# Two transformer blocks on one core: the passes of the high halves first behind each turn, merged rows turned inside a block's last quarter, the second expert's first split moved

## The chip, the core and the metric

The kernel runs on one core of a Trainium2 chip. TensorE (PE) multiplies, VectorE (DVE), ScalarE (ACT) and GpSimd (POOL) do the rest, SyncE (SP) issues nearly all loads. The metric is the device time of one execution in microseconds.

## The reference

Two blocks are computed on 256 tokens of width 1024, everything in float32. The outline of `reference()`:

```
first_block:  h = rms_norm(x); z = h @ w_in                      # 5.9k columns
              differential attention (8 heads) -> @ w_proj_a     # "pa"
              latent attention (8 heads)       -> @ w_proj_b     # "pb"
              merged = sigmoid(g_a)*y_a + sigmoid(g_b)*y_b
              x += rms_norm(merged @ w_o)                        # "wo"
              x += rms_norm((silu(h @ gate) * (h @ up)) @ down)  # FFN, 2816 wide
second_block: u = modulate(rmsnorm(h), shift, scale); z = u @ w_in_2        # "jn"
              retention -> @ w_ret_out ("ro"), sparse attention -> @ w_dsa_out ("do")
              h += g1 * ((ga*y_ret + gb*y_dsa) @ w_o)                        # "xo"
              t = modulate(rmsnorm(h)); router picks 2 of 16 experts a token
              h += g2 * sum_e gate_e * ((silu(t @ w1_e) * (t @ w3_e)) @ w2_e)
              return rmsnorm(h, norm_final_g)
```

## The kernel before, in words

**Three passes for one product.** A float32 product is made of three matmuls on rounded operands: high half of the rows by high half of the weights, high by low, low by high. `three` (L2387, L2388, L2389) issues these three side by side for each 128-row K tile. The high half of a weight unit (128 x 1024, two K tiles of 512 columns) is a copy on ACT (L986, L980), the low half a subtraction on DVE (L1522, L1517) that follows it. A unit passes through a ring of four slots; `used` counts units that PE is done with.

**A turn.** Before rows can be multiplied they are transposed: PE turns a token tile of 128 rows in two groups of four 128 x 128 transposes (L2496), ACT takes the high half out of PSUM (`rows_hi`, L1079), DVE the low half (`rows_lo`, L1657, L1659). `pairs_freed` makes PE wait until the low half is there, and `lo_ready` until the low half of the unit is. So the first product behind a turn waits for PE, ACT and DVE in a row.

**Blocks by rows.** Six places have a turn behind work that ends late. There PE takes token tile 0 through all four units first, turns the rows of tile 1 in between, and then takes tile 1 (`block_by_rows`, and `first_gate_up` for the FFN and for the first expert). The places are `x1` (start), `mg` (merged rows, block wo0), `x2` (FFN), `u` (block jn0), `mh` (merged rows, block xo0) and `v` (expert 0). The merged rows of token tile 0 are ready in the middle of block pb1 (do1), but PE turns them when this block is over.

**The order on ACT and DVE** is written by hand: each engine's program calls `split_to(n)` to say how many units are split before the next other step. It is not planned by costs, and the queues run strictly in that order. ACT before wo0 splits three units ahead and then takes the turned rows.

**The experts.** Expert 0's load is fixed; those from the second on are placed by the router's answer (`bases`), so SP issues them only when this is known. Beside expert 1's first products PE gathers the tokens of the small groups in eight steps (L2963, L2964), each into one PSUM bank: step n+1 waits until ACT has copied (L1434) and DVE has subtracted (L2296) step n. ACT and DVE work on the router (L1460 to L1463, L2245 to L2265) between the splits of the second expert's units; `L1463` is a dummy that loads the Silu table again behind the two Exp.

## Time and profile before

| | us |
|---|---|
| median of 3 runs (1011.11 to 1012.3) | 1011.11 |
| the profiled execution: its own time | 1013.72 |
| its span in the profile | 1012.1 |
| PE busy in it (92%) | 934.3 |
| DVE busy / ACT busy / POOL busy | 691.0 / 523.4 / 247.0 |

Start times in rows count from the start of the span; around the span lie 1.62 us. The two remaining views that matter are the timeline, in which a bracket behind an instruction tells how long its engine sat idle before it and what ended that, and the granted clock by stretch (1.00 is 2.4 GHz, 0.50 is 1.2 GHz).

### The profile page before, as it was taken

What the parts mean: (1) busy time and instruction counts of PE and PEld (TensorE: products, weight loads), DVE (VectorE), ACT (ScalarE), POOL (GpSimd) and SP (SyncE); (2) the same over time, 40 slices, a digit from 0 to 9 for tenths busy, and PEclk for the clock granted to TensorE, in tenths of its full rate; (3) what the DMA queues carried; (4) which work ended last, traced back from release to release, by engine and by line L of the source; (5) the groups of instructions that cost most, each with busy time, mean ns of one, the idle gap of its engine ahead of it and who ended that gap; (6) DMA issues with size and microseconds to landing.
All of it is one profiled execution on the core that took longest, in us unless ns stands there. A gap on an engine that the chain in (4) does not pass through costs nothing. (4 is left out here: it accounts for less than half of the span.)

```text
span 1012.1 us, 12623 instructions
## 1 busy us (share of the span) xinstructions
PE 934.3 (92%) x4334; PEld 748.1 (74%) x4334; DVE 691.0 (68%) x933; ACT 523.4 (52%) x814; POOL 247.0 (24%) x228
## 2 busy tenths in 40 slices
PE   4998999889998999999989998998989989999995
PEld 3886776678775888888678885686767768777774
DVE  4868467857756687878665443896667875785973
ACT  4655566665346353434444555544434464674661
POOL 3686036599522011110127000023100100000001
PEclk9999999999999999999989999898999999999998
DMA  8646846546555799997547655243235184996951
GB/s 274 202 138 187 274 119 201 166 140 214 192 167 197 254 299 325 299 325 252 165 124 201 195 168 168 91 146 105 84 110 187 56 278 143 320 317 231 325 203 41
DMA packets 116148, 199.45 MB, mean 197 GB/s; under 512 B 6361, under 2 KB 63761, under 8 KB 115841
## 3 DMA queue, kind: packets, MB, share of 16 engines
q1 hardware_dynamic: 110192, 177.00, 53.9%
q0 software_dynamic: 5904, 21.78, 6.5%
q8 instruction: 29, 0.48, 0.2%
q14 instruction: 23, 0.19, 0.1%
HBM read 197.70 MB, written 2.62 MB: 198 GB/s over the span
## 5 line engine op out<-in xcount | busy, mean ns | idle before, releaser
L1522 DVE TENSOR_TENSOR w_lo<-raw,w_hi 128x1024 fp32r<-128x1024 f32 x220 | 288.8, 1325 | 137.0 <-ACT w_hi L986 134.4
L2387 PE MATMUL lin<-w_hi,a_hi 128*128 128x512 f32 (+2 forms) x728 | 293.4, 403 | 18.3 <-DVE w_lo L1522 6.6
L986 ACT ACTIVATE w_hi<-raw 128x1024 fp32r<-128x1024 f32 x220 | 229.3, 1058 | 123.6 <-PE lin L2389 116.8
L2389 PE MATMUL lin<-w_hi,a_lo 128*128 128x512 f32 (+2 forms) x728 | 284.7, 391 | 0.0
L2388 PE MATMUL lin<-w_lo,a_hi 128*128 128x512 f32 (+2 forms) x704 | 274.7, 390 | 0.0
L2387 PEld LDWEIGHTS lin<-w_hi,a_hi 128*128 128x128 f32 x728 | 139.9, 192 | 53.1 <-issue 14.9
L2389 PEld LDWEIGHTS lin<-w_hi,a_lo 128*128 128x128 f32 x728 | 139.8, 192 | 29.4
L2388 PEld LDWEIGHTS lin<-w_lo,a_hi 128*128 128x128 f32 x704 | 135.2, 192 | 25.0
L858 POOL TENSOR_SCALAR stat<-stat 128x2 f32<-128x2 f32 (+1 forms) x31 | 11.4, 368 | 511.6 <-ACT idk_t L1099 451.9
L2496 PE MATMUL turn<-cst,arena 128*128 128x128 f32 x230 | 35.0, 290 | 22.0 <-DVE arena L1711 10.0
L2387 PE MATMUL lin<-w_hi,b_hi 128*128 128x512 f32 x114 | 46.3, 407 | 4.8 <-DVE arena L1559 2.0
L2496 PEld LDWEIGHTS turn<-cst,arena 128*128 128x128 f32 x230 | 26.8, 147 | 32.3 <-DMA cst<-in_constants_dram 7.9
L906 POOL TENSOR_SCALAR rows<-rows,c_col 128x1024 f32<-128x1024 f32 x16 | 48.8, 3049 | 2.2 <-POOL mod L907 1.5
L925 POOL DMA_DIRECT2D arena<-in_w_ada_dram x32 | 16.9, 529 | 125.1 <-DVE mod L1616 124.6
L2389 PE MATMUL lin<-w_hi,b_lo 128*128 128x512 f32 x114 | 45.2, 397 | 0.0
L907 POOL TENSOR_TENSOR mod<-mod,rows 128x1024 f32<-128x1024 f32 x16 | 41.9, 2620 | 1.3
L1616 DVE SCALAR_TENSOR_TENSOR mod<-arena,c_col,mod 128x1024 f32 x32 | 40.9, 1278 | 0.0
L1117 ACT ACTIVATE probs<-sco,stat 128x128 f32<-128x128 f32 (+1 forms) x48 | 19.6, 419 | 36.3 <-DVE stat L1681 36.3
L2388 PE MATMUL lin<-w_lo,b_hi 128*128 128x512 f32 x94 | 37.4, 398 | 0.0
L1079 ACT ACTIVATE a_hi<-turn 128x512 fp32r<-128x512 f32 x24 | 13.2, 595 | 40.8 <-PE turn L2496 40.8
L2387 PE MATMUL lin<-w_hi,arena_r 128*128 128x512 f32 x80 | 32.6, 407 | 0.0
L2389 PE MATMUL lin<-w_hi,arena_r 128*128 128x512 f32 x80 | 31.5, 394 | 0.0
(434 smaller groups left out, 1601.7 us busy)
## 6 DMA issues: line engine op xcount, KB each, us to landing
raw<-in_w_in_dram SPq DMA_DIRECT2D x76, 512.0 KB, 4.4
arena<-in_w_ada_dram POOLq DMA_DIRECT2D x32, 512.0 KB, 5.9
raw<-in_w_ffn_gate_dram SPq DMA_DIRECT2D x22, 512.0 KB, 5.0
raw<-in_w_ffn_up_dram SPq DMA_DIRECT2D x22, 512.0 KB, 6.1
raw<-in_w_ffn_down_dram SPq DMA_DIRECT2D x22, 512.0 KB, 4.0
rows<-in_w_ada_dram SPq DMA_DIRECT2D x16, 512.0 KB, 4.0
raw<-in_w_o_dram SPq DMA_DIRECT2D x16, 512.0 KB, 4.1
raw<-in_w_gate_dram SPq DMA_DIRECT2D x16, 512.0 KB, 4.0
```

The lines of the kernel that those rows point to most:

```text
L906: step(pool.tensor_scalar(early_slots[n % 3], early_slots[n % 3], c_col[:, k:k + 1], None, ALU.mult))
L907: pool.tensor_tensor(acc, acc, early_slots[n % 3], ALU.add).then_inc(ada_done, 1)
L925: pool.dma_start(ada_slots[k % 4], ada_source(k, bass.ds(i * D + 2 * D, D)))\
L986: act.activation(w_hi[:, s, :], raw[:, s, :], ACT.Copy).then_inc(hi_ready, 1)
L1079: act.activation(a_hi[:, 4 * (g % 2):4 * (g % 2) + 4, t * P:(t + 1) * P], bank_of(f"{label}.{g}").rearrange("p (k n) -> p k n", k=4), ACT. ...
L1117: i = act.activation(dst, src, ACT.Exp, bias=st("nmax", k, 1), accum_out=st("rsum", k, 1))
L1522: dve.tensor_tensor(w_lo[:, s, :], raw[:, s, :], w_hi[:, s, :].bitcast(F32), ALU.subtract)\
L1616: dve.scalar_tensor_tensor(out=acc, in0=ada_slots[k % n_s], scalar=c_col[:, k:k + 1], in1=acc, op0=ALU.mult, op1=ALU.add).then_inc(ada_don ...
L2387: pe.matmul(dst, l_hi, r_hi, start=start, stop=False)
L2388: pe.matmul(dst, l_hi, r_lo, start=False, stop=False)
L2389: return pe.matmul(dst, l_lo, r_hi, start=False, stop=stop)
L2496: i = pe.transpose(b[0:n, at:at + m], src, ident[0:m, 0:m])
```

## The change

At the places above PE issues the high-by-high passes by themselves (`unit_high`, waiting only for the high halves) and the other two passes later (`unit_rest`). `turned_block` writes this order out for the blocks behind a turn; the first block of the FFN, expert 0 (token tile 0), the product do0, expert 1 and the two last down products get the same split. The merged rows of tile 0 are turned before the last unit of pb1 (do1). Two of the four sums of shift rows move ahead of the turn of tile 1 in the FFN. On ACT and DVE `split_to` calls and the steps around them move accordingly. In expert 1 the high half of its first unit is made between the two Exp, its low half before the end of the router's arithmetic, and the table load comes after the splits of the first gate and up units.

```diff
+HI_NAMES = [n for n in TURN_NAMES if TURNS[n][1] == "dve" and n[:3] not in ("dao", "dso")]
+HI_MADE = {name: count + 1 for count, name in enumerate(HI_NAMES)}
...
             u_next = BLOCKS["wo0"][1]
-            split_to(u_next + LEAD)
+            split_to(u_next + 2)
             rows_hi("mg", 0, 0.5)
...
             rows_hi("x2", 0)
+            squares("wo.1", [lin[:, b + 1, :] for b in banks])
             split_to(u_next + 4)
-            squares("wo.1", [lin[:, b + 1, :] for b in banks])
             rows_hi("x2", 1)
+            shift_copied(0, 2)
...
             act.activation(route_x, route_x, ACT.Exp).then_inc(route_e, 1)
+            split_to(u + 1)
             act.wait_ge(route_in, 2)
             act.activation(route_y, route_y, ACT.Exp).then_inc(route_e, 1)
-            act.activation(st("route", 30, 1), st("neg_half", 0, 1), ACT.Silu)
             split_to(u + 2)
             side(0, "down")
             split_to(u + 4)
+            act.activation(st("route", 30, 1), st("neg_half", 0, 1), ACT.Silu)
...
-                split_to(u_next + 1)
+                split_to(u_next + 2)
+                rows_lo(label, 0, 0.5)
                 dve.wait_ge(used, u_next)
                 merge_rows(name, gate, 1)
-                rows_lo(label, 0, 0.5)
...
             dve.wait_ge(first_rows, 2)
+            wo_weighted(0)
             wo_rows(0)
-            split_to(u_next + LEAD - 1)
+            split_to(u_next + 2)
             rows_lo("x2", 0)
+            dve.wait_ge(used, u_next)
+            wo_weighted(1)
+            split_to(u_next + 3)
+            wo_rows(1)
             split_to(u_next + 4)
-            dve.wait_ge(used, u_next)
-            wo_rows(1)
             rows_lo("x2", 1)
...
             add_normed("ffn", 1)
+            rows_lo("u", 0)
             dve.wait_ge(x_ready, 2 * NT)
             step(gained(1, mod[:, D:2 * D]))
-            rows_lo("u", 0)
...
             first_of(per(r_em, 16), cst[:, C_W16:C_W16 + 16], 16, m)
+            split_to(gate_up_unit(1) + 1)
             dve.wait_ge(route_e, 2)
...
+                if name == "do0":
+                    if part == 0:
+                        for p in range(2):
+                            pe.wait_ge(turn_hi, HI_MADE[f"de.{p}"])
+                            for t in range(NT):
+                                unit_high(name, p, t)
+                    pairs_freed(f"de.{part}")
+                    for t in range(NT):
+                        unit_rest(name, part, t)
+                    return
...
+            def turned_block(name, label, *rows_from):
...
+                    for part in range(3):
+                        high(part, 0)
+                    rest(0, 0)
+                    rest(1, 0)
+                    high(3, 0)
+                    rest(2, 0)
+                    turn_second(label, *rows_from)
+                rest(3, 0)
+                high(0, 1)
+                high(1, 1)
+                for part in range(4):
+                    rest(part, 1)
+                    if part < 2:
+                        high(part + 2, 1)
...
-            block_by_rows("pb1")
-            turn_first("mg", NT + 1, gate1, merged)
-            block_by_rows("wo0", "mg", NT + 1, gate1, merged)
+            block_by_rows("pb1", lambda: turn_first("mg", NT + 1, gate1, merged))
+            turned_block("wo0", "mg", NT + 1, gate1, merged)
...
+                            if (t, half) == (0, 1):
+                                shift_sums(0, 2)
+                                turn_second(rows_label, count)
                             pairs_freed(f"{rows_label}.{2 * t + half}")
...
+                    if p == 1:
+                        for t in range(NT):
+                            gate_up_high(t, u, half)
                     pe.wait_ge(lo_ready, u + 2 * half + 2)
```

What this does on PE between block pb1 and block wo0 (`turn` is the turned merged rows, `mod` their source, `arena_r` the left operand of pb1, `a_hi` and `a_lo` that of wo0). Before, from the end of pb1:

```order
L2387 MATMUL lin<-w_hi,arena_r 128x512
L2388 MATMUL lin<-w_lo,arena_r 128x512
L2389 MATMUL lin<-w_hi,arena_r 128x512
L2496 MATMUL turn<-cst,mod 128x128 x8
L2387 MATMUL lin<-w_hi,a_hi 128x512
L2388 MATMUL lin<-w_lo,a_hi 128x512
L2389 MATMUL lin<-w_hi,a_lo 128x512
```

Now, from the same turn:

```order
L2578 MATMUL turn<-cst,mod 128x128 x8
L2399 MATMUL lin<-w_hi,arena_r 128x512
L2400 MATMUL lin<-w_lo,arena_r 128x512
L2401 MATMUL lin<-w_hi,arena_r 128x512
L2399 MATMUL lin<-w_hi,arena_r 128x512
L2400 MATMUL lin<-w_lo,arena_r 128x512
L2401 MATMUL lin<-w_hi,arena_r 128x512
L2470 MATMUL lin<-w_hi,a_hi 128x512 x6
L2479 MATMUL lin<-w_lo,a_hi 128x512
L2480 MATMUL lin<-w_hi,a_lo 128x512
```

Six matmuls of pb1 stand behind the turn now, and six passes that need only high halves come before the first low one.

On ACT beside the router: `stat` is the router's row, `w_hi<-mod` are the high halves of expert 1's first four units, `arena_r<-turn` is the copy of the first gathered step, `mod<-lin` the scaled result of expert 0. Before:

```order
L1460 ACT_TABLE_LOAD
L1460 ACTIVATE stat<-stat 128x8
L1462 ACTIVATE stat<-stat 128x2
L1463 ACT_TABLE_LOAD
L1463 ACTIVATE stat<-stat 128x1
L980 ACTIVATE w_hi<-mod 128x1024 x2
L1434 ACTIVATE arena_r<-turn 128x384
L980 ACTIVATE w_hi<-mod 128x1024 x2
L1474 ACTIVATE mod<-lin,stat 128x512 x2
```

Now:

```order
L1465 ACT_TABLE_LOAD
L1465 ACTIVATE stat<-stat 128x8
L984 ACTIVATE w_hi<-mod 128x1024
L1468 ACTIVATE stat<-stat 128x2
L984 ACTIVATE w_hi<-mod 128x1024
L1439 ACTIVATE arena_r<-turn 128x384
L984 ACTIVATE w_hi<-mod 128x1024 x2
L1472 ACT_TABLE_LOAD
L1472 ACTIVATE stat<-stat 128x1
L1480 ACTIVATE mod<-lin,stat 128x512 x2
```

One split has moved ahead of the second Exp, and the table load from before four splits to behind them.

## Rows read from the trace of the kernel before

**Rows 1.** The page, busy time of the engines: us, share, instructions.

```profile
PE 934.3 (92%) x4334; PEld 748.1 (74%) x4334; DVE 691.0 (68%) x933; ACT 523.4 (52%) x814; POOL 247.0 (24%) x228
```

**Rows 2.** The waits, PE: in total, times, longest (us).

```profile
PE lin L2387 <- DVE a_lo L1657: 6.3, 3, 2.2
```

**Rows 3.** The timeline of PE, wo0, wo1: start, length, instruction, [idle before].

```profile
281.34 0.47 PE L2387 MATMUL lin<-w_hi,a_hi 128*128 128x512 f32 x1 [1.28 <-issue]
...
286.69 0.48 PE L2387 MATMUL lin<-w_hi,a_hi 128*128 128x512 f32 x1
...
304.56 1.09 PE L2496 MATMUL turn<-cst,arena 128*128 128x128 f32 x8
```

**Rows 4.** The timeline of PE and DVE, from the FFN to block jn0.

```profile
507.10 1.24 PE L2496 MATMUL turn<-cst,arena 128*128 128x128 f32 x8 [2.01 <-DVE arena L1716]
...
510.49 0.77 PE L2387 MATMUL lin<-w_hi,a_hi 128*128 128x512 f32 x1 [2.14 <-DVE a_lo L1657]
...
512.68 1.28 DVE L1716 SCALAR_TENSOR_TENSOR arena<-arena,stat,mod 128x1024 f32<-128x1024 f32 x1 [0.72 <-POOL stat L859]
...
516.66 1.03 PE L2496 MATMUL turn<-cst,arena 128*128 128x128 f32 x8
```

**Rows 5.** By stretch: busy PE, PEld, DVE, ACT, POOL; granted clock; DMA.

```profile
743.50:746.80 3.30, 3.30 (x9) 2.65 (x8) 1.29 (x2) 0.00 (x0) 0.00 (x0) 0.50 0.39 134
815.20:818.50 3.30, 3.30 (x9) 2.52 (x9) 3.19 (x7) 3.30 (x6) 0.00 (x0) 0.50 1.11 365
```

**Rows 6.** The timeline of DVE, block in0.

```profile
27.51 2.40 DVE L1522 TENSOR_TENSOR w_lo<-raw,w_hi 128x1024 fp32r<-128x1024 f32 x2
```

**Rows 7.** The timeline of PE and ACT, the FFN's first products.

```profile
307.63 0.47 PE L2387 MATMUL lin<-w_hi,a_hi 128*128 128x512 f32 x1 [1.97 <-DVE a_lo L1657]
...
314.15 1.10 PE L2496 MATMUL turn<-cst,arena 128*128 128x128 f32 x8 [2.12 <-DVE arena L1711]
...
321.50 1.28 ACT L1246 ACT_TABLE_LOAD   x1
...
321.92 1.88 PE L2555 MATMUL sco<-mod,ones 128*128 128x512 f32 x4
...
326.00 0.60 PE L2724 MATMUL turn<-cst,arena 128*128 128x128 f32 x4
```

**Rows 8.** The timeline of PE, the FFN's last down product.

```profile
495.92 0.50 PE L2387 MATMUL lin<-w_hi,b_hi 128*128 128x512 f32 x1 [1.41 <-DVE b_lo L1931]
```

**Rows 9.** The timeline of PE at block do0.

```profile
743.17 0.53 PE L2387 MATMUL lin<-w_hi,b_hi 128*128 128x512 f32 x1 [2.01 <-DVE arena L1559]
```

**Rows 10.** The timeline of PE, expert 0.

```profile
786.35 0.47 PE L2387 MATMUL lin<-arena_r,a_hi 128*128 128x512 f32 x1 [2.20 <-DVE a_lo L1657]
...
790.84 1.25 PE L2496 MATMUL turn<-cst,arena 128*128 128x128 f32 x8 [0.28 <-DVE arena L1716]
```

**Rows 11.** The timeline of SP, ACT, PE and DVE, expert 1's first half.

```profile
803.92 0.39 SPq L709 DMA_DIRECT2D mod<-in_w_exp_gate_dram  x1
...
810.10 1.28 ACT L1463 ACT_TABLE_LOAD   x1
...
811.50 1.99 ACT L980 ACTIVATE w_hi<-mod 128x1024 fp32r<-128x1024 f32 x2
...
814.99 0.70 PE L2387 MATMUL lin<-w_hi,a_hi 128*128 128x512 f32 x1 [3.22 <-DVE mod_r L1517]
...
817.94 1.93 ACT L980 ACTIVATE w_lo<-arena 128x2048 fp32r<-128x2048 f32 x1
...
822.63 0.55 DVE L2296 TENSOR_TENSOR arena_r<-turn,arena_r 128x384 fp32r<-128x384 f32 x1
...
823.23 0.45 PE L2963 MATMUL turn<-arena_r 128*128 128x384 f32 x1 [0.16 <-DVE arena_r L2296]
```

**Rows 12.** DMA issues from 800 to 816 us: median us from issue to landing.

```profile
mod<-in_w_exp_gate_dram SPq DMA_DIRECT2D x2, 512.0 KB, 5.2
...
rows<-in_w_exp_up_dram SPq DMA_DIRECT2D x1, 512.0 KB, 9.9
```

156 lines of the change are left out of this document (118 added, 38 removed).

## The prediction, written before the changed kernel ran

> **What bounds the kernel now.** I read the page first: PE is busy for 934.3 of 1012.1 us [rows 1], so PE bounds the kernel, and an edit can only win what PE does not do in the other 78 us, or what it does at half clock. Then the waits of PE: the longest lines are not loads but single steps of the chain turn, high half, low half, as the wait for `a_lo` with 3 cases and 6.3 us [rows 2]. Then the timeline at each turn, for what stands before and behind the wait, and last the granted clock around it. One matmul of 512 columns costs 0.229 us in a stream: 78 of them lie between 286.69 and 304.56 [rows 3]. At half clock it is 0.43 us: 18 between 510.49 and 516.66 took 6.17 us in place of 4.12, because most of them ran at the lower level [rows 4], and a busy stretch of 3.3 us at 0.50 did 9 [rows 5].
>
> The number of matmuls does not change; each edit is priced by how much earlier PE passes the place. Where PE streams before and after a place, loads and splits follow PE's `used` count and DVE's splits, so they shift with it, and a gain is kept.
>
> **Part by part.**
>
> Start (x1). PE's order gains some tenths, but the next block needs the low half of its first unit, and DVE makes that at 27.51 [rows 6] behind small work for tables that hangs on squares and loads, not on PE. I take 0; bounds 0 and 0.5 (two passes at 0.229 moved past the turn).
>
> Merged rows (mg, wo0). Before, PE sat 1.28 us at 281.34, and from there to 286.69 it did 18 matmuls (4.12) and one turn (0.8 without its tail; the row at 304.56 gives 1.09 with it) in 5.35, so another 0.4 was waiting [rows 3]. Now six matmuls, 1.4 us, lie behind the turn, and six high passes, 1.4 us, before the first low one. In these 2.8 us ACT makes two halves and DVE two differences of 0.6 each, which fit. The merge of tile 1 on DVE (2 x 0.7) comes behind them and is wanted only by the turn 20 passes later. So the whole 1.7 us goes. The lower bound is 1.0, if the third unit's split on ACT, now behind the turned rows, holds the sixth high pass. The same place in the second block (mh, xo0) has the same 1.28 us idle; merged(0) comes 0.3 us late for the earlier turn but the rest covers it: 1.6, at least 0.8.
>
> FFN's first products (x2). PE idles 1.97 us for the low half and 2.12 for the rows of tile 1 [rows 7]. The high passes fill the first, but the rows of tile 1 hang on squares, a POOL power and DVE, and I get their turn only 1.0 us earlier; the fourth unit's low half now comes behind them (0.4 of wait again). What counts is that two of the four sums, 1.88 us at 321.92 [rows 7], move into the wait at 314.15. Next in line is the table load at 321.50 that ends at 322.78, plus four instructions of 256 columns (0.4 each, estimated from 1.28 for 1024 columns [rows 4]), with the load 0.4 earlier than now: the turn of 326.00 can go at 324.3. I take 1.7; bounds 0.4 (only the load's shift) and 2.4.
>
> The last down products. Both wait 1.41 us for `b_lo` [rows 8] (two places, the second at 996.46). Four high passes (0.9) start when ACT's copy is there, one DVE difference (0.7) before the low half: 0.7 each; bounds 0.4 and 0.9.
>
> Rows u (jn0). PE waits 2.01 us for the modulated rows, which stays, then 2.14 us for `a_lo`, and runs the first part at half clock until 516.66 [rows 4]. With the highs at once PE starts 2.1 us earlier, at 508.4. The next bound is the modulated row of tile 1, 512.68 + 1.28 = 513.96. At full clock 20 passes end at 513.0 and the turn goes at 514.0, with 20 passes done where before 18 were done at 516.66: 2.66 + 0.46, less 0.35 for the fourth unit's low half, 2.75. With the clock falling exactly as before it is 1.1. The remaining idle is half as long, so a shorter low stretch is likely: I take 2.3.
>
> do0. PE idles 2.01 us because DVE evacuates block ro1 before `b_lo` [rows 9]; now eight high passes (1.8 us) need only ACT, which leaves 0.4 idle: 1.6. Behind the idle time PE was busy for a low stretch, 3.3 us at 0.50 [rows 5], which costs half of itself, 1.65. With 0.4 idle it should not come; I take 1.4 of it: 3.0; bounds 0.7 and 3.3.
>
> Expert 0 (v). The 2.20 us at 786.35 is filled in part, but the turn of tile 1 at 790.84 waits for DVE's rows [rows 10], so only the four extra high passes are won, 0.9. The router's arithmetic behind it is DVE's and not moved: I take 0.5; bounds 0 and 0.9.
>
> Expert 1. PE idles 3.22 us until 814.99 for `mod_r`, the low half whose high half ACT starts at 811.50 [rows 11]. Now the highs start at 811.3 and the lows at 813.8. But the eight gathers share one PSUM bank, and the third one waits for ACT and DVE. Their work is only re-ordered: of ACT's 1.28 us table load none goes away, it stands now before expert 0's result. I get ACT's pair of splits from 817.94 to 817.7, and then 1.93 for it, 2.4 for DVE's pair [rows 6] and 0.55 for the gather's difference (as at 822.63): the third gather at 822.6 in place of 823.23 [rows 11], 0.7 with the 0.5 of expert 0 in it. PE, being faster, arrives there at 818.2 and idles 4.3 us in one piece. Before, the 3.22 us were followed by a stretch at 0.50 from 815.2 to 818.5 [rows 5], and the wait at the third gather was still only 0.16 [rows 11]: that low stretch lay in DVE's shadow. The next one lies behind the third gather, where PE is what all wait for: half of 3.3, 1.65. Both experts together: 0.7 - 1.65 = -1.0; bounds -2.0 (a low stretch longer by one half) and +1.1.
>
> Here the split of three passes has a price that the trace must rule out. PEld counts 4334 loads for 4334 matmuls [rows 1]: each matmul has a load of its own already, so taking the two products of one left tile apart adds none. The Trainium skill (TensorE: Matmul & The Clock Gate, "What a matmul computes" and the step LDWEIGHTS) describes the load as its own instruction so that one load may serve many matmuls; by that rule some 120 left tiles would be loaded a second time. The trace disagrees for this kernel.
>
> The moved table load: the load at 810.10 takes 1.28 and ends at 811.38, the next activations come right behind, the split at 811.50 [rows 11]. No other cost shows. The Trainium skill (ScalarE: Activation LUTs, "What ACT_TABLE_LOAD costs") adds a drain of about 1380 ns to 1283 ns for a switch. By it the load in its new place would hold expert 0's result for longer; a mechanism of that kind is the fourth rival.
>
> **The sum.** 0 + 1.7 + 1.6 + 1.7 + 0.7 + 0.7 + 2.3 + 3.0 - 1.0 = 10.7 us off the profiled execution of 1013.72, which gives 1003.0. That execution stands 2.6 above the median of 1011.11, for which I have no cause in the program; the change of 10.7 is taken off the median: 1000.4.
>
> **The rivals.**
>
> 1. The clock spares expert 1 and block jn0: +1.65 and +0.45: 998.3. For it: after 1.97 and 2.12 us of idle time at 307.63 and 314.15 matmuls ran on at their usual step; against it: 3.22 us was followed by a low stretch.
> 2. The waits only move: DVE and ACT have their strict order, and behind the highs PE waits for the same low halves. Then the filled waits of x2 and u give nothing, since their ends hang on the rows of tile 1: without 1.7, 2.3 and half of do0's 3.0 the sum is 5.2: 1005.9. For it: five of the places end on DVE. Against it: the loss at half clock in [rows 4].
> 3. It does not do what it says: every high pass won is waited away before the low ones, since units' low halves come at DVE's rate, 2.4 us for two [rows 6], against 2.7 us that PE needs for one of twelve passes. PE is the slower, so I give little: 1010.5.
> 4. The table load costs as much again as its row shows, 1.28 us [rows 11], at a place where it stands between matmul results that ACT must fetch; the third gather comes that much later: 1001.7. Against it: at 810.10 nothing shows behind it.
> 5. Slower: expert 1's loads arrive late. SP issues them at 803.92, and the first split now stands before the second Exp in ACT's queue; behind it are queued the second Exp, on which the router's gates on DVE wait, the gather's copy and expert 0's result. The median landing of such a load is 5.2 us, 809.1, at most 0.4 late. But the slowest in the stretch took 9.9 [rows 12]: 813.8, 5.1 later than 808.7, when ACT would be free; this passes to the gathers, 4.4 after slack, with 2.5 of half clock. It decides from a landing later than 809.4 on. With the other terms at their lower ends (1.0 + 0.8 + 0.4 + 0.8 + 1.1 + 0.7 = 4.8) the kernel is 2.1 slower: 1013.2.
> 6. Slower by the weights: each of the 120 parted passes shows its load, 748.1 / 4334 = 0.17 us [rows 1], 20 in all: 1020.8. With loads hidden as now, nothing.
>
> **How the numbers follow.** Forecast 0.5 (1000.4, own range 998.9 to 1003), rival 1 0.15, rival 2 0.18, rival 3 0.04, rival 4 0.05, rival 5 0.05, rival 6 0.03. The range reaches from 997.5, below rival 1, to 1006, with rival 2 in it; outside are rivals 3, 5 and 6 and the tails, under 0.2. A measurement of this kernel can tell 0.2%, 2 us, from no change. Faster by more than 2 us are the forecast and rivals 1, 2 and 4: 0.88. Within it is rival 3 with half of rival 5: 0.06. Slower are the other half and rival 6: 0.06.
>
> **What would show it.** PE's idle time before the first product of wo0 and xo0 is gone (1.28 before). The turn of tile 1 in jn0 stands 2 to 3 us nearer to the turn of tile 0, and no low stretch follows do0. The hidden rows' first turn in the FFN comes right behind two sums, not four. Most telling is expert 1: a wait of about 4 us before the third gather, with a low stretch behind it, and a wait of 0.5 before the first low pass. Were there no wait, or an ACT queue that waits for a load before the second Exp, my order of events there would be wrong. If the total moves by less than 5 us although these waits are gone, the claim that a gain is kept through the streams is wrong.

## The result, and the profile after

The changed kernel took 1001.52 us (median of 4 runs, 1001.07 to 1003.31) against 1011.7 us for the kernel before on the same chip (4 runs, 1011.11 to 1013.55): ratio 0.9893, 95% interval 0.9879 to 0.9907. Forecast were 1000.4 us and a range from 997.5 to 1006.0. On a second chip it took 999.98 against 1013.81, ratio 0.9859 (0.9843 to 0.9875). The profiled execution took 1001.17 us with a span of 999.5, against 1013.72 and 1012.1 before. So the gain is 10.2 us by the medians of the first chip, 13.8 by those of the second, and 12.55 by the two profiles. Why these differ is a part of the finding.

From the page of the changed kernel, the busy time of the engines, which answers to [rows 1]:

```profile
PE 932.6 (93%) x4334; PEld 745.4 (75%) x4334; DVE 689.2 (69%) x933; ACT 523.1 (52%) x814; POOL 247.0 (25%) x228
```

There are as many matmuls and loads of left tiles as before, 4334 each, and both are busy for no longer. Taking the passes apart cost no load.

The timeline of PE after the change (start, length, instruction, [idle before, and what ended it]), from the merged rows to the FFN's hidden rows; it answers to [rows 3] and [rows 7]:

```profile
277.83 1.03 PE L2578 MATMUL turn<-cst,mod 128*128 128x128 f32 x8
...
280.10 1.53 PE L2470 MATMUL lin<-w_hi,a_hi 128*128 128x512 f32 x6
...
302.88 1.09 PE L2578 MATMUL turn<-cst,arena 128*128 128x128 f32 x8
304.48 1.17 PE L2776 MATMUL lin<-w_hi,a_hi 128*128 128x512 f32 x4 [0.51 <-ACT a_hi L1083]
...
308.60 1.88 PE L2637 MATMUL sco<-mod,ones 128*128 128x512 f32 x4
...
322.38 0.66 PE L2823 MATMUL turn<-cst,arena 128*128 128x128 f32 x4 [0.81 <-DVE arena L1921]
```

Six matmuls stand between the turn and the first high passes of wo0 (278.62 to 280.10), and none of the 1.28 us of idle time is left. The turn of the FFN's rows comes 1.68 us earlier than before, with 0.21 us lost ahead of the place: the step gave 1.89. Two of the four sums, 1.88 us, now stand at 308.60, where PE would wait for the rows of tile 1, and only two are left ahead of the hidden turn. PE's wait of 1.97 us before the first product of the FFN is one of 0.51 for the high half. The hidden turn comes 3.62 earlier, so the FFN's step gave 1.94.

The same view at u and jn0, which answers to [rows 4]:

```profile
502.79 1.09 PE L2578 MATMUL turn<-cst,arena 128*128 128x128 f32 x8 [2.00 <-DVE arena L1722]
504.33 1.62 PE L2470 MATMUL lin<-w_hi,a_hi 128*128 128x512 f32 x6 [0.45 <-ACT a_hi L1083]
...
509.85 1.09 PE L2578 MATMUL turn<-cst,arena 128*128 128x128 f32 x8 [0.62 <-DVE arena L1722]
```

The wait of 2.14 us for `a_lo` is now one of 0.45 for the high half, and the turn of tile 1 follows 7.06 us behind that of tile 0, where it was 9.56.

By stretch (length; busy PE, PEld, DVE, ACT, POOL; granted clock, DMA share, GB/s), in the kernel before behind the turn of u:

```profile
508.00:514.60 6.60, 4.46 (x12) 3.29 (x11) 5.81 (x7) 3.94 (x7) 1.41 (x2) 0.50 0.18 48
```

And in the changed kernel, behind the turn of u and behind that of de, where before had 0.50 in the first line of [rows 5]:

```profile
508.00:512.00 4.00, 3.34 (x18) 2.38 (x17) 3.25 (x4) 1.09 (x2) 0.47 (x1) 1.00 0.43 133
...
736.00:740.00 4.00, 4.00 (x20) 3.27 (x19) 2.42 (x4) 1.33 (x2) 0.00 (x0) 1.00 0.40 139
```

The timelines in expert 1 answer to [rows 11]. ACT:

```profile
803.38 1.28 ACT L1472 ACT_TABLE_LOAD   x1
804.67 0.20 ACT L1472 ACTIVATE stat<-stat 128x1 f32<-128x1 f32 x1
```

PE there:

```profile
803.54 0.50 PE L3007 MATMUL lin<-mod_r,a_hi 128*128 128x512 f32 x1 [0.79 <-DVE mod_r L1523]
...
811.91 0.44 PE L3086 MATMUL turn<-arena_r 128*128 128x384 f32 x1 [3.67 <-DVE arena_r L2308]
...
822.34 0.66 PE L3153 MATMUL turn<-cst,arena 128*128 128x128 f32 x4 [0.95 <-DVE arena L2290]
```

DVE, with the pair's split and behind it the difference that the third gather waits for:

```profile
809.10 2.29 DVE L1523 TENSOR_TENSOR arena_r<-arena,w_lo 128x2048 fp32r<-128x2048 f32 x1 [0.36 <-ACT w_lo L984]
811.31 0.55 DVE L2308 TENSOR_TENSOR arena_r<-turn,arena_r 128x384 fp32r<-128x384 f32 x1
```

And the granted clock behind the third gather, by stretch:

```profile
812.40:815.70 3.30, 3.30 (x10) 2.73 (x9) 0.60 (x2) 2.29 (x2) 0.00 (x0) 0.50 0.99 315
```

This is the event that the prediction called the most telling. The wait of 3.22 us before the first product is gone, one of 0.79 stands before the first low pass, PE then stands 3.67 us at the third gather, and the stretch behind it runs at the lower level. The split ahead of the table load ends at 803.37, the row of the load shows 1.28 us from 803.38, and the next instruction starts at 804.67, 1.29 behind that start: no more than this is paid. The Trainium skill (ScalarE: Activation LUTs, "What ACT_TABLE_LOAD costs") would add a drain of some 1380 ns to a switch; the trace does not agree here, at either place of the load.

How much earlier PE passes each place, by the two profiles (us):

| behind | earlier | the step gave | forecast |
|---|---|---|---|
| start | -0.21 | -0.2 | 0 |
| mg, wo0 | 1.68 | 1.89 | 1.7 |
| x2, FFN's first products | 3.62 | 1.94 | 1.7 |
| FFN's last down product | 4.31 | 0.74 | 0.7 |
| u, jn0 | 6.85 | 2.54 | 2.3 |
| attention, nothing changed | 6.38 | -0.47 | 0 |
| do0 and mh, xo0 | 10.33 | 3.95 | 4.6 |
| expert 0 | 10.84 | 0.51 | 0.5 |
| expert 1 | 9.77 | -1.07 | -1.5 |
| experts 2 to 15, nothing changed | 11.82 | 2.05 | 0 |
| last down product | 12.57 | 0.74 | 0.7 |

The steps are read at the place itself; between two places the streams shift by some hundredths, so the columns need not add up to the last digit.

### The profile page after: what moved, and what is told of

Same layout as the page of the kernel before. It is cut to its first block and busy times, and to the rows that moved or that the text cites. A ratio compares the mean times of both kernels' runs of the same rounds, so it can differ in the third digit from the quotient of the medians.

```text
span 999.5 us, 12650 instructions
## 1 busy us (share of the span) xinstructions
PE 932.6 (93%) x4334; PEld 745.4 (75%) x4334; DVE 689.2 (69%) x933; ACT 523.1 (52%) x814; POOL 247.0 (25%) x228
## 5 line engine op out<-in xcount | busy, mean ns | idle before, releaser
L2399 PE MATMUL lin<-w_hi,a_hi 128*128 128x512 f32 (+2 forms) x632 | 252.6, 400 | 3.5 <-DVE w_lo L1528 1.7
L2401 PE MATMUL lin<-w_hi,a_lo 128*128 128x512 f32 (+2 forms) x632 | 246.1, 389 | 0.0
L2400 PE MATMUL lin<-w_lo,a_hi 128*128 128x512 f32 (+2 forms) x624 | 242.3, 388 | 0.0
L2399 PEld LDWEIGHTS lin<-w_hi,a_hi 128*128 128x128 f32 x632 | 120.8, 191 | 31.1 <-issue 3.2
L2401 PEld LDWEIGHTS lin<-w_hi,a_lo 128*128 128x128 f32 x632 | 120.5, 191 | 25.0
L2400 PEld LDWEIGHTS lin<-w_lo,a_hi 128*128 128x128 f32 x624 | 119.4, 191 | 22.3
L2399 PE MATMUL lin<-w_hi,b_hi 128*128 128x512 f32 x98 | 39.3, 401 | 0.0
L2401 PE MATMUL lin<-w_hi,b_lo 128*128 128x512 f32 x98 | 38.3, 391 | 0.0
L2400 PE MATMUL lin<-w_lo,b_hi 128*128 128x512 f32 x82 | 31.9, 389 | 0.0
```

Source lines behind the costliest of these rows:

```text
L2399: pe.matmul(dst, l_hi, r_hi, start=start, stop=False)
L2400: pe.matmul(dst, l_hi, r_lo, start=False, stop=False)
L2401: return pe.matmul(dst, l_lo, r_hi, start=False, stop=stop)
```

## The experiments

Two theories were to be told apart. **Theory A:** each step is worth what its own place shows, the idle time filled and the stretch of half clock that goes with it, and the stream behind keeps it. **Theory B:** the waits only move, and most of the gain is somewhere else (phases of the clock, landings of the loads). Most parts (not the start, expert 0 and the last down products) were taken out of the changed kernel, wo0 and xo0 together and the others one at a time; one was put into the kernel before by itself, and expert 1, where the change costs time, was built in several ways.

### The kernel before once more (e0_before_again)

No edit.

> The kernel before once more, for how far one profiled execution stands from another. In the two profiles the changed kernel gains 2.05 us between the turns of expert 1 and of the last expert (9.77 at the first, 11.82 at the last), where nothing was changed and TensorE waits for DVE six times behind loads that land late. If that is chance of the loads' landing, this profile's length between the two turns (832.11 to 994.44, 162.33 us) differs from the first by 1 us or more; if it is a gain of the change, it agrees within 0.3.

It took 1013.41 us. From the hidden turn of expert 1 to that of the last expert it needed 159.98 us (834.14 to 994.12), where the first profile of the same kernel needed 162.33; that is 2.35 us between two executions of one kernel, as much as the 2.05 us in the row "experts 2 to 15" of the table. The waits of ACT over these experts (in total, times, longest, us), in the first profile of the kernel before:

```profile
ACT w_lo L980 <- DMA raw<-in_w_exp_up_dram: 3.6, 2, 2.2
```

And in the second:

```profile
ACT w_lo L980 <- DMA raw<-in_w_exp_up_dram: 2.0, 2, 1.2
```

The same loads land later in one execution than in the other, and the splits wait for them; PE's own waits for hidden rows there are 5.9 us in the first and 3.9 in the second. That the landings cause the difference is read from these rows and not tested, but it is there without any edit. So those 2.05 us are no part of what the change does.

The experts are not the only such place. Against the first profile, the second loses 1.5 us up to the merged rows and 1.6 at the FFN's first products, and wins 0.4 at jn0 and 0.6 in attention. The two executions agree within 0.3 us only because these differences cancel.

### Expert 1 as before (e1_expert1_as_before)

```diff
-            split_to(u + 1)            # ACT, ahead of the second Exp; on DVE likewise
+            act.activation(st("route", 30, 1), st("neg_half", 0, 1), ACT.Silu)   # before the gates
...
-            act.activation(st("route", 30, 1), st("neg_half", 0, 1), ACT.Silu)   # behind the splits
...
-                    if p == 1:
-                        for t in range(NT):
-                            gate_up_high(t, u, half)
```

> The changed kernel with expert 1 as before: three passes side by side on TensorE, the table load and the splits on ACT and DVE in their old order. In the changed kernel TensorE idles 3.67 us before the third gather (at 811.91) and the first passes behind it run at half clock. Theory (the early passes are paid back by the clock): the turn of expert 1's hidden rows, 822.34 in the changed kernel, comes at about 821.3, the wait before expert 1's first product is 3.2 us again with the low stretch behind it and nothing idle at the third gather; the time is 1.0 us less than the changed kernel's 1001.5, so 1000.5. Rival (the early passes are a gain of their own): the turn comes 2 us or more later, 1003.5.

997.49 us (996.89 to 1002.07), ratio 0.985 (0.9823 to 0.9877). The timeline of PE:

```profile
798.53 0.34 PE L3084 MATMUL turn<-arena_r 128*128 128x384 f32 x1
...
802.61 0.56 PE L2397 MATMUL lin<-w_hi,a_hi 128*128 128x512 f32 x1 [3.21 <-DVE mod_r L1522]
...
819.72 0.66 PE L3145 MATMUL turn<-cst,arena 128*128 128x128 f32 x4 [0.96 <-DVE arena L2288]
```

From the first gather to the hidden turn it takes 21.19 us, as in the kernel before (21.19, 21.21 in its second profile); the changed kernel takes 22.26. This part of the change costs 1.07 us: the sign, the place and the mechanism are as forecast. The wait of 3.21 us is followed by the lower level here too (0.50 from 803.00 to 806.20), but PE then still waits 0.15 us for DVE at the third gather, so this stretch costs nothing.

The median lies 3.0 us under the forecast of 1000.5, which comes from elsewhere: in the profile 1.96 us are won in attention, where nothing was changed (see f1 below), and 1.19 in experts 2 to 15.

### More for PE before the third gather, and the gathers first (e2, e3)

The first variant puts the high passes of the second half of expert 1 before the third gather. The second puts the copies and differences of the gathered rows before the splits of expert 2 on both engines.

```diff
# e2_second_highs_before_gather
-                    if p == 1:
+                    if p == 1 and half == 0:
                         for t in range(NT):
                             gate_up_high(t, u, half)
...
+                        if p == 1 and kt == 3:
+                            for t in range(NT):
+                                gate_up_high(t, u, 1)
                         side(p - 1, kt)
# e3_gathers_first, ACT and DVE
+            side(0, 1)                 # before expert 0's result
...
-            for kt in (1, 3, 5):
-                split_to(u + AHEAD - 1 + kt // 2)
-                side(0, kt)
+            side(0, 3)
+            split_to(u + AHEAD + 1)
+            side(0, 5)
```

> The changed kernel, but the eight high passes of expert 1's second half stand before the third gather, in the 3.67 us in which TensorE idles. Theory (idle time in one piece, then half clock): the idle time falls to 1.8, no low stretch follows, the third gather stays where it is (811.9), and the turn of expert 1's hidden rows comes 3.3 us earlier (1.85 for the passes moved, 1.5 for the clock), at 819.0; the time is 998.2. Rival 1 (only the passes are won, the clock falls all the same): 1.85, 999.7. Rival 2 (ACT and DVE bound the whole stretch, TensorE's gain is waited away at the fourth gather): within 0.5 of the changed kernel.

997.74 us (994.92 to 999.96), ratio 0.9838 (0.9813 to 0.9864). First gather to hidden turn: 18.86 us, 3.40 less than the changed kernel, against 3.3 forecast and 1.85 by the first rival. The idle time at the third gather is 1.86 (forecast 1.8).

> The changed kernel, but ACT copies and DVE subtracts the second gather before expert 0's result, the gates by choice and the pair of splits for expert 2, and the third before that pair. Theory (the third gather waits for order, not for work): the idle time of 3.67 us before the third gather goes to under 0.5, no low stretch, the turn of expert 1's hidden rows comes 4 us earlier, at 818; the time is 997.5. Rival (the work is only moved on): the pair of splits for expert 2, now late, makes TensorE wait before expert 2's first product, and less than 1 us is left of the gain, 1000.5 or more.

995.78 us (994.59 to 996.02), ratio 0.9819 (0.9798 to 0.9841): 17.24 us from gather to hidden turn, 5.02 less than the changed kernel, where 4 was forecast. The wait at the third gather is gone. PE in the first of the two (e2):

```profile
811.45 0.44 PE L3086 MATMUL turn<-arena_r 128*128 128x384 f32 x1 [1.86 <-DVE arena_r L2308]
...
817.67 0.44 PE L3086 MATMUL turn<-arena_r 128*128 128x384 f32 x1 [0.84 <-DVE arena_r L2308]
```

PE in the second (e3):

```profile
815.23 0.44 PE L3088 MATMUL turn<-arena_r 128*128 128x384 f32 x1 [1.35 <-DVE arena_r L2309]
```

The longest idle piece here is 1.86 us in the first and 1.35 in the second, and the clock stays high behind them in both (1.00 from 811.6 to 815 and from 812 to 816). So here shorter idle pieces saved the half clock as well as the wait. But about 1.1 us is given back: expert 2 takes 21.31 and 21.32 us in place of 20.23, with a wait of 1.29 and 1.31 us for a gathered group, since what was put off is now waited for. That is the rival of e3 in kind, at a fifth of the gain.

### The changed kernel again (f1_after_again)

No edit; the kernels below ran on the same chip.

> The changed kernel itself, so that the kernels beside it are compared with it on one chip. Expected 0.989 of the kernel before. Its first profile took 2 us longer from the first turn of the value weights (604.27) to the first gather (800.08) than the three variants of expert 1 did, 195.81 against 193.73 to 193.86, though they run the same code there. Theory A: that is the phase of the granted clock and of the loads, and differs from profile to profile; this profile then shows between 193.7 and 196. Rival: it belongs to the changed kernel and comes back as 195.8.

999.98 us (998.74 to 1001.13), ratio 0.9859 (0.9843 to 0.9875). From the value weights to the first gather it needed 195.83 us, as in its first profile (195.81), where e1, e2, e3 and f2 needed 193.73 to 193.86 with the same code there, and f5 and g4 195.47 and 195.37. The rival's number came back, and it lies in theory A's range as well, so this run alone decides nothing; f5 and g4 show that the time is not of the changed kernel alone. It is not evenly spread either. Two stretches make it, in which nothing was changed. The view by stretch of the changed kernel, its first profile:

```profile
634.00:642.00 8.00, 7.27 (x18) 5.24 (x19) 6.98 (x17) 4.85 (x7) 0.00 (x0) 0.57 0.19 68
705.00:710.00 5.00, 4.81 (x19) 3.78 (x18) 1.92 (x8) 2.31 (x6) 1.14 (x2) 0.66 0.31 105
```

The same view of the variant with expert 1 as before (e1):

```profile
634.00:642.00 8.00, 6.81 (x23) 5.17 (x24) 6.91 (x19) 4.90 (x8) 0.00 (x0) 0.79 0.22 68
705.00:710.00 5.00, 4.81 (x26) 3.93 (x26) 2.03 (x9) 2.98 (x7) 1.15 (x2) 1.00 0.33 105
```

The granted clock falls behind the waits in attention in every profile, but for a shorter or a longer stretch. I found nothing in the programs that decides it.

### Expert 2's gathered rows ahead of its splits too (f5_gathers_ahead)

```diff
# on top of e3, ACT and DVE
-            split_to(u + AHEAD + 1)
+            split_to(u + AHEAD)
             side(0, 5)
...
+                    if p == 1:
+                        side(p, kt)
                     split_to(u + 1 + kt // 2)
-                    side(p, kt)
+                    if p > 1:
+                        side(p, kt)
```

> The variant in which the gathers of expert 1 stand before its low passes (995.78 us, 17.24 us from the first gather to the hidden turn of expert 1) gave 1.09 us back in expert 2, where TensorE waited 1.35 and 1.31 us. Here VectorE and ScalarE also make the gathered rows of expert 2 (copy and subtraction) ahead of the splits of its weights. Theory A: the two waits are for those gathered rows, which stand behind splits on VectorE; with the rows ahead both waits go, expert 2 takes 20.2 us instead of 21.32, and the time is 1 to 2.5 us under that variant, 993.3 to 994.8. Theory B: VectorE and ScalarE are full over this stretch, and the work that is put back (the splits) is waited for instead: 0.5 us or less is gained, or up to 1 us lost, and waits for split halves of the weights stand in place of the two.

998.16 us (994.99 to 1000.34), ratio 0.9839 (0.9822 to 0.9857). Theory B is what came, with a larger loss than its 1 us. DVE:

```profile
817.62 2.29 DVE L1527 TENSOR_TENSOR raw_r<-raw,w_lo 128x2048 fp32r<-128x2048 f32 x1 [1.32 <-ACT w_lo L984]
```

PE:

```profile
820.75 1.08 PE L3161 MATMUL turn<-cst,arena 128*128 128x128 f32 x4 [3.01 <-DVE arena L2294]
```

The two waits for gathered rows are gone. But the split of DVE now comes later, because it first waits 1.32 us for ACT, and the hidden rows of expert 1 stand behind it. PE waits 3.01 us for them, and the clock falls again. From the first gather to the hidden turn of expert 2 it takes 40.16 us, against 38.56 in e3. What PE waits for is not a split half, as theory B had it, but the hidden rows behind one.

### One split of both engines behind the fourth gathered group (g4_one_split_later)

```diff
# on top of e3, ACT and DVE
             side(0, 3)
-            split_to(u + AHEAD + 1)
             side(0, 5)
+            split_to(u + AHEAD + 1)
```

> The variant in which the gathers of expert 1 stand before its low passes (995.78 us), with one split of both engines moved behind the fourth gathered group of expert 1. There TensorE waited 1.35 us for that group, which VectorE made behind a split of 2.28 us. Theory A: the wait goes and the hidden rows of expert 1 are made no later: 1.0 to 1.3 us under that variant from the first gather to the hidden turn (16.0 instead of 17.24 us). Theory B, which the variant with the gathers of expert 2 ahead bears out (there the hidden rows came behind a split that had itself waited for ScalarE, and TensorE waited 3.0 us): the split comes late, the hidden rows behind it, and the stretch takes 18 us or more, some 0.5 to 2 us over that variant in the median.

999.49 us (998.89 to 1000.4), ratio 0.9865 (0.985 to 0.988). From the first gather to the hidden turn it takes 21.01 us, where theory A had 16.0 and theory B 18 or more. So it is theory B again, beyond its range, with one move only. ACT:

```profile
812.72 0.49 ACT L1439 ACTIVATE arena_r<-turn 128x384 fp32r<-128x384 f32 x1 [3.78 <-PE turn L3089]
```

PE:

```profile
820.45 1.11 PE L3155 MATMUL turn<-cst,arena 128*128 128x128 f32 x4 [5.22 <-DVE arena L2291]
```

ACT has its strict order: with the copy of the fourth group at its head it stands idle for 3.78 us, for a turn that PE makes later, and the splits are late by that. The wait of 1.35 us is gone, and one of 5.22 stands at the hidden turn, where e3 has none.

### Block jn0 as before, and jn0 alone (f2_u_off, g2_u_alone)

```diff
# f2, on the changed kernel
             add_normed("ffn", 1)
-            rows_lo("u", 0)
             dve.wait_ge(x_ready, 2 * NT)
             step(gained(1, mod[:, D:2 * D]))
+            rows_lo("u", 0)
...
-                turned_block(first, label, rows_count)
+                (turned_block if label == "x1" else block_by_rows_turned)(first, label, rows_count)
# g2, on the kernel before: the same two places the other way round
-                block_by_rows(first, label, rows_count)
+                (turned_block if label == "u" else block_by_rows)(first, label, rows_count)
```

`block_by_rows_turned` in f2 and f4 is the old `block_by_rows` with its turn inside.

> The changed kernel with block jn0 (behind the turn of u) as before: its product units by token half in the old order and the low half of u made after the splits that it had stood behind. All else as in the changed kernel. The step came out 2.54 us shorter in the comparison of the two profiles, in which before had a stretch of half clock here. Theory A: the idle times of 2.0 and 2.1 us come back and with them 2.3 to 2.6 us over the changed kernel. Rival: only the clock phase differed, and without a low stretch the step is worth 1.1 us. Second rival: later parts absorb it, within 0.5 us of the changed kernel.

1005.11 us (1002.96 to 1008.89), ratio 0.9918 (0.9899 to 0.9937), 5.1 above the changed kernel (999.98 on this chip), and so above theory A's 2.3 to 2.6 as well as above the rivals.

> The kernel before with one step of the change alone: block jn0 behind the turn of u in the new order, and the low half of u made ahead of the step that it had stood behind. The same step taken out of the changed kernel cost 3.45 us at the place itself and 5.1 us in the medians. Theory A (a step is worth what its place shows, the rest is where the stretches of half clock and the loads fall): 2.3 to 3.4 us earlier behind jn0, and a median 1 to 4 us under the kernel before. Theory B (a step is worth the whole 5.1 us because later parts build on it): 4.5 us or more under the kernel before.

1010.98 us (12 runs, 1008.31 to 1014.32) against 1013.42, ratio 0.9975 (0.9964 to 0.9987). PE in f2:

```profile
502.92 1.09 PE L2594 MATMUL turn<-cst,arena 128*128 128x128 f32 x8 [2.01 <-DVE arena L1722]
506.30 0.77 PE L2399 MATMUL lin<-w_hi,a_hi 128*128 128x512 f32 x1 [2.28 <-DVE a_lo L1663]
...
513.31 1.03 PE L2594 MATMUL turn<-cst,arena 128*128 128x128 f32 x8
```

PE in g2:

```profile
510.45 1.09 PE L2566 MATMUL turn<-cst,arena 128*128 128x128 f32 x8 [2.01 <-DVE arena L1720]
511.99 1.63 PE L2452 MATMUL lin<-w_hi,a_hi 128*128 128x512 f32 x6 [0.45 <-ACT a_hi L1083]
...
517.51 1.09 PE L2566 MATMUL turn<-cst,arena 128*128 128x128 f32 x8 [0.61 <-DVE arena L1720]
```

From turn to turn f2 needs 10.39 us and g2 needs 7.06, the very number of the changed kernel. Across the block f2 loses 3.4 us against the changed kernel, and g2 gains 2.58 on the first profile of the kernel before (2.54 by the first comparison). On the second profile of the kernel before, whose low stretch here is shorter, g2 gains 2.2. So the step alone is worth 2.2 to 2.6 us in the stream and 2.4 in the medians. Taken out it costs more, because the stretch of half clock comes back whole. The view by stretch of f2:

```profile
508.40:512.00 3.60, 3.60 (x10) 2.74 (x10) 2.42 (x2) 0.00 (x0) 0.06 (x1) 0.50 0.48 148
```

The 14 passes from 506.30 to 512.39 lie 0.43 us apart here. In the first profile of the kernel before, the clock was already at 0.50 from 508.0 on (the stretch is shown above), so that the wait of 2.14 us before the first pass at 510.49 [rows 4] lay in it.

The new order does not rule out a fall. In five of the eleven profiles that have it (f3, f4, f5, g1, g4) the lower level follows the wait of 2.0 us before the turn of u, for 3.4 us, and costs 0.3 to 0.4 us.

### The merged rows as before (f4_merged_off)

```diff
-            block_by_rows("pb1", lambda: turn_first("mg", NT + 1, gate1, merged))
-            turned_block("wo0", "mg", NT + 1, gate1, merged)
+            block_by_rows("pb1")
+            turn_first("mg", NT + 1, gate1, merged)
+            block_by_rows_turned("wo0", "mg", NT + 1, gate1, merged)
...
# do1, xo0 and mh likewise; on ACT and DVE split_to and rows_lo in the old order
```

> The changed kernel with wo0 and xo0 (behind the merged rows of the two blocks) as before: the merged rows turned after the block, not in its last quarter, the units in the old order, and the splits and low halves of ScalarE and VectorE in the old order. All else as in the changed kernel. Theory A: the sum of the two steps, 1.89 and 1.41 us in the comparison of profiles, comes back, 3.3 us over the changed kernel (2.8 to 3.8). Rival: these waits were partly moved on to later weights (a wait for w_lo grew from 0.94 to 1.40 us in the changed kernel), then 1.5 to 2.5 us. Second rival: under 1 us, if the gains in the profiles were phases of the clock.

1006.01 us (1004.46 to 1007.57), ratio 0.9921 (0.9906 to 0.9935), 6.0 above. PE:

```profile
283.18 0.47 PE L2399 MATMUL lin<-w_hi,a_hi 128*128 128x512 f32 x1 [1.28 <-issue]
...
750.70 0.47 PE L2399 MATMUL lin<-w_hi,a_hi 128*128 128x512 f32 x1 [1.28 <-issue]
...
768.14 0.50 PE L2399 MATMUL lin<-w_hi,a_hi 128*128 128x512 f32 x1 [0.95 <-DVE w_lo L1528]
```

Both idle times of 1.28 us are back. In the stream the block wo0 costs 1.90 us (against f1, 1.21 later ahead of it, 3.11 behind), which is the 1.89 of the comparison. The block xo0 costs only 0.64, so theory A's 3.3 is missed and the first rival (1.5 to 2.5) is nearest with 2.54 for both. The changed kernel shows why:

```profile
745.43 1.09 PE L2578 MATMUL turn<-cst,arena 128*128 128x128 f32 x8 [0.55 <-DVE arena L1585]
...
765.20 0.50 PE L2399 MATMUL lin<-w_hi,a_hi 128*128 128x512 f32 x1 [1.40 <-DVE w_lo L1528]
```

PE waits 0.55 us for the merged rows of tile 0, which the earlier turn now reaches before DVE has them, and it meets the wait for `w_lo` further on with 1.40 us, where it is 0.95 here and 0.94 in the kernel before. The 1.7 us of idle time and waiting that wo0 gave back, less 0.55 and 0.45, are 0.7.

### Block do0, and the FFN's first products, as before (f3_do0_off, g1_x2_off)

```diff
# f3
-                if name == "do0":
-                    if part == 0:
-                        for p in range(2):
-                            pe.wait_ge(turn_hi, HI_MADE[f"de.{p}"])
-                            for t in range(NT):
-                                unit_high(name, p, t)
...
# g1, first_gate_up, and shift_sums(0, 4) behind it; squares, weightings and copies of ACT and DVE in the old order
-                                pe.matmul(dst, a_hi[:, kt, c], rl, start=False, stop=False)
-                                i = pe.matmul(dst, a_lo[:, kt, c], rh, start=False, stop=kt == DK - 1)
+                                i = three(lin[:, t, :].rearrange("p (a n) -> p a n", a=2), a_hi[:, kt, c],
+                                          a_lo[:, kt, c], rh, rl, kt == 0, kt == DK - 1)
```

> The changed kernel with block do0 (behind the turn of de) as before: its four units each with three passes side by side, so that nothing is multiplied until the first low half is made. All else as in the changed kernel. Theory A: the idle time of 2.0 us and the stretch of half clock behind it come back: 2.5 us over the changed kernel by the comparison of the two profiles, 3.0 by the sum of the prediction; and since the variant without the merged-row edits lost only 0.64 us at xo0 where the comparison gave 1.41, the rest of what came at these two blocks belongs here, so 3.3 us at most. Rival: block xo0 behind it, which waits 1.40 us for a split of its weights, swallows part: 1.0 to 1.5 us less waiting there, and 1.5 to 2.0 us in all.

1004.54 us (1004.4 to 1005.18), ratio 0.9919 (0.9906 to 0.9932), 4.6 above. PE at do0:

```profile
736.75 0.57 PE L2399 MATMUL lin<-w_hi,b_hi 128*128 128x512 f32 x1 [2.01 <-DVE arena L1565]
...
748.28 1.09 PE L2568 MATMUL turn<-cst,arena 128*128 128x128 f32 x8
```

Two stretches of the same kernel:

```profile
736.00:740.00 4.00, 3.25 (x8) 2.60 (x9) 2.38 (x4) 0.37 (x1) 0.00 (x0) 0.62 0.40 140
784.00:788.00 4.00, 3.87 (x13) 2.71 (x12) 3.76 (x5) 3.96 (x5) 0.00 (x0) 0.59 0.02 4
```

The idle time of 2.01 us is back with the half clock behind it, 2.89 us in the stream (against f1, 0.46 earlier ahead of it, 2.43 later behind): theory A. Up to the merged rows' turn it is 3.3; there 0.4 comes back, because the row at 748.28 has no wait, where the changed kernel has 0.55 at this turn (745.43, shown above). Another 1.6 comes at 784, behind a wait of 1.70 us in expert 0 that the changed kernel has as well (1.69), without a fall of the clock.

> The changed kernel with the first gate and up products of the FFN (behind the turn of x2) as before: three passes side by side, the four shift sums after them, and the squares, weightings and shift copies of ScalarE and VectorE in the old order. All else as in the changed kernel. Theory A: the idle times of 1.97 and 2.12 us come back; the step was worth 1.94 us in the comparison of profiles (1.7 in the prediction), so 1.7 to 2.2 us over the changed kernel at the first hidden turn of the FFN. Rival: part of it came from the merged rows being turned earlier, whose splits then stood ahead, and the step alone is worth 1.2 us or less. Over the whole kernel up to 2 us may be added or taken by where the stretches of half clock fall later on, as in the two variants before.

1003.76 us (1000.77 to 1004.02), ratio 0.9899 (0.9881 to 0.9917), 3.8 above. PE:

```profile
303.38 1.09 PE L2572 MATMUL turn<-cst,arena 128*128 128x128 f32 x8
306.45 0.47 PE L2393 MATMUL lin<-w_hi,a_hi 128*128 128x512 f32 x1 [1.97 <-DVE a_lo L1662]
...
312.98 1.09 PE L2572 MATMUL turn<-cst,arena 128*128 128x128 f32 x8 [0.58 <-DVE arena L1716]
...
324.83 0.60 PE L2809 MATMUL turn<-cst,arena 128*128 128x128 f32 x4
```

From the rows' turn to the hidden turn it takes 21.45 us, before 21.44 [rows 3, 7], after 19.50. In the stream behind, g1 is 1.85 later. At the place itself this is theory A as forecast.

The same block in the second profile of the kernel before takes 23.05 us from turn to turn, 1.61 more than in the first. The waits are the same (1.97 and 2.13), but behind the second one the lower level follows, where PE is what all wait for:

```profile
315.60:318.80 3.20, 3.20 (x12) 2.91 (x13) 1.32 (x2) 1.85 (x3) 0.00 (x0) 0.50 0.03 11
```

In g2, which has the old code here as well, it does so too. In g1 itself the lower level stands behind the first wait, 3.3 us at 0.50 from 307.6 on, and costs nothing: only 0.58 us are then waited for the rows of tile 1, in place of 2.12. So this step is worth 1.9 us or 3.5, by where the clock falls in the kernel that it is compared with.

### Why a part taken out costs more in the median than at its place

| taken out | at its place | over f1, the two profiled executions | over the changed kernel, medians |
|---|---|---|---|
| jn0 | 3.4 | 3.65 | 5.1 |
| wo0 and xo0 | 2.54 | 5.57 | 6.0 |
| do0 | 2.89 | 3.27 | 4.6 |
| FFN's first products | 1.85 | 2.89 | 3.8 |

The four medians sum to 19.5 us, more than the whole change is worth on that chip. The profiles show where a part of the rest goes. The wait of some 3.7 us at the third gather is the same in all, but in three of them (all but do0) the lower level lasts twice as long as the 3.3 us at 0.50 shown for the changed kernel. The view by stretch of f2:

```profile
812.80:819.50 6.70, 6.04 (x15) 5.08 (x16) 3.12 (x4) 2.29 (x2) 0.00 (x0) 0.50 0.68 216
```

The same view of f4:

```profile
814.10:820.80 6.70, 5.92 (x15) 4.96 (x16) 3.12 (x4) 2.29 (x2) 0.00 (x0) 0.50 0.70 223
```

From the first gather to the hidden turn these three take 23.49, 23.45 and 23.54 us, against 22.26 and 22.25 in the two profiles of the changed kernel: 1.2 us. Experts 2 to 15 take 159.7 us in the second profile of the changed kernel and 159.7 to 161.7 in the four. And the second profile of the changed kernel was the slowest of its four runs, 1.15 above their median. Attention works the other way: it takes 1.3 to 2.0 us less in f2, f4 and g1 than in the changed kernel, and 0.3 less in f3. What is left is within the spread of single executions (up to 6 us for f2). With one trace for each kernel it can't be split further, so that the medians of these four bear out the order of size and not the price of each part.

## Why the prediction was right

**The range and the middle.** On the first chip 1001.52 lies 1.1 above the forecast. The sum of the terms was 10.7; the medians gave 10.2 and, on the second chip, 13.8. By the profiles the parts that were priced gave 11.2, and 1.4 came where nothing was changed (2.05 in the experts, less 0.47 and 0.21). So the sum was right within 0.6 us, but that closeness is partly luck: single places were off by up to 1 us with both signs, and which profile of the kernel before is taken moves the FFN's step alone by 1.6.

**wo0, 1.7:** 1.89 by the comparison, 1.90 by f4. The idle time and the 0.4 us of waiting were read rightly.

**xo0, 1.6:** the term that was mis-sized. f4 measured 0.64. The idle time of 1.28 us is the same as at wo0, and I took it for kept; but a wait for `w_lo` behind it, which the trace before shows with 0.94 us, grew to 1.40, and a new wait of 0.55 us stands before the earlier turn. The prediction saw the second ("0.3 us late") and let the rest cover it, which it did not; the first it did not have. This is where "a gain is kept through the streams" did not hold. The rule needs a stream without a wait on DVE in it.

**do0, 3.0:** 2.89 by f3. As forecast it is in two parts of nearly one size: the idle time falls from 2.01 to 0.30, and the stretch of half clock behind it, 3.3 us at 0.50, is gone. In the comparison do0 and xo0 gave 3.95 together, by f3 and f4 3.53. The difference is the wait for the merged rows, 0.55 us with both parts in and none shown with do0 out.

**x2, 1.7:** 1.94 and 1.85, and 3.5 against the second profile of the kernel before. The prediction took from the first profile that matmuls ran on at their usual step behind these waits; that was the luck of one execution. **Last down products, 0.7 each:** 0.74 each, seen in the comparison only, not by an experiment.

**jn0, 2.3:** 2.54, and 2.58 alone in the kernel before. The bet on the clock (2.75 without the low stretch, 1.1 with all of it) came out near its upper end, because the clock did not fall there in either profile of the changed kernel; in five variants it did.

**Experts 0 and 1, -1.0:** -0.56. Expert 0 gave 0.51 of 0.5. The third gather was won 0.48 us over the first (the forecast had 0.2), the half clock cost 1.55 of 1.65. The prediction's order of events was right as far as its last row, with a wait of 3.67 us for the 4.3 forecast and of 0.79 for 0.5 before the first low pass.

**The rivals.** That the clock spares expert 1 (1) did not come: 0.50 from 812.4 on. That the waits only move (2) is true of a part of xo0 and nowhere else among the parts tried. That the high passes win nothing (3) is ruled out by every one of them. The table load (4) cost its row and no more. Loads of expert 1 (5) came in time: the splits start at 797.78 without a wait on a load. No load was added (6): PEld counts 4334 as before, in 745.4 us.

**What the prediction lacked** is a bound for what is not in the change: the same kernel differs by 2.35 us in the experts and by 1.6 at the FFN's first products from one execution to the next, and kernels with the same code in attention differ by some 2 us there.

## What to carry to other kernels

Look behind a turn for passes that need only the first result of the chain, and price the place by the idle time and by the stretch of half clock behind it; the second can be as large as the first. Then look down the same block for the next wait on the other engines, since what is won is kept only up to there. Where an engine with a strict order serves two customers, move one item at a time and ask what its head then waits for: g4 turned a wait of 1.35 us into one of 5.22 with a single move. And before a part is priced to tenths of a microsecond, take a second profile of the same kernel.

The best kernel of the study is e3: 995.78 us, 0.9819 of the kernel before on its chip, 17.24 us in place of 22.26 in expert 1.

## What the runs showed of the hardware

Idle times of 2.0 to 2.3 us were followed by the lower level of the clock (0.50) in several places and not in others. Before do0 it followed in all four profiles that have that wait. At the FFN's first products the old code waits 1.97 us and then 2.12: the lower level followed neither in the first profile of the kernel before, the second wait in its second profile and in g2, and in g1 (where the second wait is 0.58) the first. At expert 0 it followed a wait of 2.20 us in the first profile of the kernel before and not one of 2.17 in the second. A wait of 1.70 us in f3 was followed by it, one of 1.69 in the changed kernel was not. Behind the waits of 3.0 to 5.2 us in expert 1 it came each time.

Between the first 30 us and the last expert, each low stretch lasted either 3.4 or 6.8 us, in all 14 profiles. The same wait of 3.7 us brought the short one in both profiles of the changed kernel (1.55 us of loss) and the long one in three variants (1.2 more). So the fall can be foreseen at a place with three microseconds of idle time or more, its length only as one of these two, and what it costs depends on whether PE is what all wait for behind it.
